# FFN's first quad on Trainium2: VectorE's weight sums moved ahead of f's last three channel blocks, the fourth low part moved ahead of the next sums

## The chip, the cores and the metric

The program runs on one core of a Trainium2 chip. The metric is the device time of one execution in microseconds. Each engine (TensorE, VectorE, ScalarE, GpSimd, and SyncE, which issues the DMAs) has its own queue of instructions, worked in order; semaphores tie the queues together. TensorE's clock is granted at one of two levels, 1.2 and 2.4 GHz.

## The reference, cut to what matters

The reference is a transformer block (latent attention beside an mLSTM, an FFN, a gated embedding) and a second block with a pooling mixer, all in float32, for 1024 tokens of width 1024. The change lies in the FFN of the first block:

```
f = rms_norm(h, ffn_pre_norm)                       # 1024 x 1024
f = (silu(f @ w_gate) * (f @ w_up)) @ w_down        # hidden width 2816 = 11 groups of 256
h = h + rms_norm(f, ffn_post_norm)
```

## The kernel before, in words

**Precision.** Every float32 matrix is used as a high part (rounded by a copy to TensorE's format, fp32r) and a low part (the value less its high part). A product is three matmuls, high x high, high x low, low x high (`three`, line 1356 for all its matmuls). A tile named `_hi` or `_lo` is such a part; `ring_hi`, `ring_lo` are eight slots of weight blocks.

**Strassen's scheme.** The FFN's first two matrix products go by groups of 256 hidden columns: a gate part and an up part for each. Group 0 is done plainly (`whole_quad`, four banks of 24 matmuls, for gate and again for up). From group 1 on each part is a "quad" of seven products in the Winograd form of Strassen's scheme (`quad`), 12 matmuls each: product o takes weight block o from ring slot o and the operand `factors[o]`, which is a quarter of f or one of four sums of quarters, `f_sum[0]` to `f_sum[3]`. Products 0, 4 and 5 use quarters of f, products 1, 2, 3 and 6 use the sums 1, 0, 2 and 3. Each quad also needs four sums of weight quarters (`w_sum`), one for each of its products 1, 2, 3 and 5. The prediction counts products and blocks of a quad from 1 to 7; in the code they are o = 0 to 6.

**Who does what around the change (some 495 to 550 us).** TensorE does group 0's two whole quads, then without a break the gate quad of group 1 and its up quad. VectorE first computes the f sums, in four channel blocks k = 0 to 3: four sums high + low (line 3179), then `f_raw[0]`, `[2]`, `[1]`, `[3]` of that block (lines 3190 to 3195). ScalarE copies the high parts of sums 1, 0, 2 block by block (line 2375), 12 copies in all, and once bank 6 of the whole quads is full the high part of `f_raw[3]` in one copy of 2048 columns (line 2380). The low parts, 2048 columns each, are shared: GpSimd has that of sum 2 (line 1243), VectorE those of sums 1, 0 (line 3203) and 3 (line 3212). All wait for ScalarE's 12 copies or the thirteenth.

VectorE's order is: f's sums for k = 0 to 3; `weight_sums(2, 0)`, the four weight sums of the gate quad (lines 3163 to 3168, each 512 columns); low parts 1 and 0; `weight_sums(3, 1)`, those of the up quad; the first two of group 0's four products silu(gate) x up, which read a PSUM bank (line 3208); low part 3; the other two products; then the sums over the gate quad's own banks (`quad_sums`). `weight_sums` waits for the raw weights' DMA (`raw_in`), and the first of them also until the last rows of f have been transposed, since it writes where these lay.

GpSimd's order is: the low part of sum 2, then for the gate quad block after block (`product_blocks`): a high part (line 1211) and a low part (line 1212) of 512 columns each into a ring slot, when the slot is free and, for a summed block, when its sum is done. Then the up quad's blocks, and so on. The ring's slots are freed by TensorE's whole quads.

TensorE waits ahead of product o of a quad for weight block o (`w_split`), for the gate quad of group 1 also for a count of low parts (`fs_split`), and from the fifth product on for ScalarE's copy of the bank that it adds to. ScalarE's first such copy (line 2385) waits for all four low parts, since it writes where `f_raw[3]` lay. SyncE stores the four products of group 0 to memory when they are done and loads the next raw weights when GpSimd has split the blocks of the last ones.

Of the kernel before, what the change touches and what calls it, by code (L numbers as in the profile page):

```python
# [18 lines left out]
F32 = mybir.dt.float32  # L19
# [3 lines left out]
ALU = mybir.AluOpType  # L23
# [61 lines left out]
def build(nc, a, out):  # L85
    ctx = ExitStack()
    with ctx:
# [10 lines left out]
        def at(name, shape, offset, dt=F32):  # L98
            return nc.alloc_sbuf_tensor_at(name, shape, dt, offset=base + offset)
# [20 lines left out]
        def col(n):  # L120
# [117 lines left out]
            for j, name in enumerate(("e_buf", "d_t", "inter", "s_t", "q_in", "k_w")))  # L238
# [12 lines left out]
        f_sum = [(at(f"fs_hi{i}", [P, 4, HALF], o, F32R), at(f"fs_lo{i}", [P, 4, HALF], o + 8 * KB, F32R))  # L251
                 for i, o in enumerate(f_sum_at)]
        f_raw = [at(f"fs_raw{i}", [P, 4, HALF], o + 8 * KB) for i, o in enumerate(f_sum_at)]
# [132 lines left out]
        fs_raw, fs_hi_ready, fs_split = map(sem, ("fs_raw", "fs_hi_ready", "fs_split"))  # L386
# [49 lines left out]
        US_SUMS, US_PARTS, US_ROWS = 16, 4, 0  # L436
# [154 lines left out]
        def raw_landed(t):  # L591

            return 32 if t == 0 else 32 * (t // 2) if t % 2 == 0 else 32 * ((t - 1) // 2 + 2)
# [2092 lines left out]
        def dve_program(dve):  # L2686
            v = nc.vector
            own = dve_own
# [470 lines left out]
            def block_sums(q, dst, t):  # L3159

                s = [dst[:, i, :].rearrange("p (k n) -> p k n", k=4) for i in range(4)]
                w00, w01, w10, w11 = (wblock(t, c, k) for c in range(2) for k in range(2))
                v.tensor_tensor(s[0], w10, w11, ALU.add).then_inc(w_summed, 1)
                dve.wait_ge(w_summed, IN_SUMS + 4 * q + 1)
                v.tensor_tensor(s[1], s[0], w00, ALU.subtract).then_inc(w_summed, 1)
                v.tensor_tensor(s[2], w00, w10, ALU.subtract).then_inc(w_summed, 1)
                dve.wait_ge(w_summed, IN_SUMS + 4 * q + 2)
                v.tensor_tensor(s[3], w01, s[1], ALU.subtract).then_inc(w_summed, 1)

            def weight_sums(t, r):  # L3170

                dve.wait_ge(raw_in[1 - r], IN_LANDED + raw_landed(2 + r) + 32 * ((t - 2 - r) // 2))
                if r == 0:
                    dve.wait_ge(rows_full, 16 + 2 * TB)
                block_sums(t - 2, w_sum[r], 2 + r)
# [7 lines left out]
            for k in range(4):  # L3183
# [13 lines left out]
                    own.mark(ins)  # L3197
                else:
                    ins.then_inc(fs_raw, 1)
            weight_sums(2, 0)  # L3200
            dve.wait_ge(fs_hi_ready, US_PARTS + 12)
            for i in (1, 0):
                v.tensor_tensor(f_sum[i][1][:], f_raw[i][:], f_sum[i][0][:].bitcast(F32), ALU.subtract).then_inc(fs_split, 1)
            weight_sums(3, 1)
            for j, b in enumerate((2, 3, 0, 1)):
                dve.wait_ge(std_full, 5 + j)
                dve.wait_ge(silu_ready, b + 1)
                v.tensor_tensor(hid_pair[0][:, b, :], ps[:, 4 + b, :], silu_g[:, b, :], ALU.mult).then_inc(hid_ready, 1)
                if j == 1:
                    dve.wait_ge(fs_hi_ready, US_PARTS + 13)  # L3210
                    dve.wait_ge(own.sem, own.at)
                    v.tensor_tensor(f_sum[3][1][:], f_raw[3][:], f_sum[3][0][:].bitcast(F32), ALU.subtract).then_inc(fs_split, 1)

            def quad_sums(q, bank0, copies, dst, sums=None, times=None, first=None, low=None):

# [489 lines left out]
        @block.vector  # L3705
        def _(dve):
            dve_program(dve)
# [30 lines left out]
```

## Time and profile before

| | us |
|---|---|
| median of 3 runs | 1812.74 (1812.66 to 1813.11) |
| the profiled execution | 1813.23 |
| its span, first to last instruction | 1811.4 |
| TensorE busy | 1791.5 (99%) |
| VectorE busy | 1405.5 (78%) |
| GpSimd busy | 1087.2 (60%) |
| ScalarE busy | 691.2 (38%) |

The rows further down name PE for TensorE, PEld for its weight loads, DVE for VectorE, ACT for ScalarE, POOL for GpSimd and SPq for SyncE's DMA queue. A timeline row has the start in us, the recorded length in us (of all instructions merged in the row, xN), engine, line, operation, output tiles <- input tiles with their shapes, and in brackets how long the engine stood idle before and who released it. An instruction's recorded length includes time in which it is held up after its start. Ends of matmuls are modelled: 0.39 us are recorded where the next one starts 0.23 later.

### The profile page before, as it was taken

To read this page: it belongs to the slowest core of one execution; us is meant where nothing else is said; L and a number is where in the kernel's file an instruction comes from. 1 tells how busy PE (TensorE), PEld (TensorE's weight loads), DVE (VectorE), ACT (ScalarE), POOL (GpSimd) and SP (SyncE) were. 2 spreads that over 40 slices of the span, in tenths; PEclk is the share of its full clock that TensorE was granted. 3 is DMA by queue.
4 is the path that set the end of the run, shared out by engine and by line. 5 is a ranking of instruction groups with operands and counts; after the bars stand their busy time and mean duration, and the time that the engine had idled before them with its cause. 6 is when DMAs were issued, how large, how long until landed. Compare 5 with 4: busy or idle time off the path is not lost.

```text
span 1811.4 us, 22601 instructions
## 1 busy us (share of the span) xinstructions
PE 1791.5 (99%) x8518; PEld 1499.4 (83%) x8518; DVE 1405.5 (78%) x1624; ACT 691.2 (38%) x1213; POOL 1087.2 (60%) x766
## 2 busy tenths in 40 slices
PE   9999999999999999999999999999999999999998
PEld 8888888888888888888888888888888888888887
DVE  7889866666696758666599989578888875798897
ACT  6545577843321111111243334415433343333313
POOL 4066632260359988888778878632665465567554
PEclk9999999999999999999999999999999999999999
DMA  7342410032303323243374631113332231943222
GB/s 208 97 150 56 136 23 20 15 129 93 123 29 105 117 82 117 69 140 117 105 278 175 232 128 47 47 47 119 114 117 105 105 139 71 365 168 108 75 97 93
DMA packets 126974, 206.54 MB, mean 114 GB/s; under 512 B 32129, under 2 KB 88065, under 8 KB 123153
## 3 DMA queue, kind: packets, MB, share of 16 engines
q1 hardware_dynamic: 126690, 205.03, 33.0%
q8 instruction: 68, 1.11, 0.2%
q14 instruction: 40, 0.33, 0.1%
q10 hardware_dynamic: 176, 0.07, 0.0%
HBM read 151.51 MB, written 53.04 MB: 113 GB/s over the span
## 4 chain that ended last, share of the span: by engine, by line
PE 72%; DVE 5%; POOL 1%; issue 1%; ACT 1%; DVEq 0%; POOLq 0%
PE ps L1356 64%; PE ps L1705 2%; PE ps L1707 2%; PE ps L1706 2%; DVE y L3609 1%; PE ps L1945 1%; PE ps L1943 1%; PE ps L1944 1%; POOL ring_lo L1212 1%; POOL ring_hi L1211 0%; DVE y L3602 0%; PE ps L1820 0%; DVE xs_lo L3436 0%; PE ps L1692 0%; PE ps L1584 0%
## 5 line engine op out<-in xcount | busy, mean ns | idle before, releaser
L1356 PE MATMUL ps<-f_hi,ring_hi 128*128 128x512 f32 x384 | 149.7, 390 | 1.3 <-POOL ring_lo L1212 1.3
L1356 PE MATMUL ps<-f_hi,ring_lo 128*128 128x512 f32 x384 | 149.4, 389 | 0.0
L1356 PE MATMUL ps<-f_lo,ring_hi 128*128 128x512 f32 x384 | 149.4, 389 | 0.0
L1290 POOL TENSOR_TENSOR ring_lo<-w_sum,ring_hi 128x512 fp32r<-128x512 f32 x60 | 94.4, 1584 | 50.9 <-ACT ring_hi L2512 50.9
L1212 POOL TENSOR_TENSOR ring_lo<-w_sum,ring_hi 128x512 fp32r<-128x512 f32 x80 | 117.9, 1473 | 6.7
L1356 PE MATMUL ps<-d_w_hi,d_hid_hi 128*128 128x512 f32 x312 | 121.5, 390 | 0.3 <-DVE hid L3302 0.3
L1356 PE MATMUL ps<-d_w_hi,d_hid_lo 128*128 128x512 f32 x312 | 121.4, 389 | 0.0
L1356 PE MATMUL ps<-d_w_lo,d_hid_hi 128*128 128x512 f32 x312 | 121.4, 389 | 0.0
L2385 ACT ACTIVATE f_copy<-ps 128x512 f32<-128x512 f32 x60 | 35.4, 597 | 221.2 <-PE ps L1356 202.4
L1356 PE MATMUL ps<-xs_hi,ring_hi 128*128 128x512 f32 x256 | 100.0, 391 | 1.5 <-DVE xs_lo L3436 1.4
L1356 PE MATMUL ps<-xs_lo,ring_hi 128*128 128x512 f32 x256 | 99.6, 389 | 0.0
L1356 PE MATMUL ps<-xs_hi,ring_lo 128*128 128x512 f32 x256 | 99.6, 389 | 0.0
L1356 PE MATMUL ps<-fs_hi,ring_hi 128*128 128x512 f32 x240 | 93.5, 390 | 0.0
L1356 PE MATMUL ps<-fs_lo,ring_hi 128*128 128x512 f32 x240 | 93.4, 389 | 0.0
L1356 PE MATMUL ps<-fs_hi,ring_lo 128*128 128x512 f32 x240 | 93.4, 389 | 0.0
L1211 POOL TENSOR_SCALAR ring_hi<-w_sum 128x512 fp32r<-128x512 f32 x80 | 72.7, 908 | 32.1 <-PE ps L1356 31.5
L1211 POOL TENSOR_SCALAR ring_hi<-stage 128x512 fp32r<-128x512 f32 x38 | 33.2, 874 | 89.4 <-PE ps L1707 83.3
L1356 PEld LDWEIGHTS ps<-f_hi,ring_hi 128*128 128x128 f32 x384 | 72.1, 188 | 16.9 <-POOL ring_lo L1212 1.9
L1356 PEld LDWEIGHTS ps<-f_hi,ring_lo 128*128 128x128 f32 x384 | 72.1, 188 | 15.0
L1356 PEld LDWEIGHTS ps<-f_lo,ring_hi 128*128 128x128 f32 x384 | 72.1, 188 | 14.9
L1290 POOL TENSOR_TENSOR ring_lo<-stage,ring_hi 128x512 fp32r<-128x512 f32 x24 | 35.4, 1475 | 76.0 <-ACT ring_hi L2512 76.0
L1094 POOL TENSOR_TENSOR w_lo<-stage,w_hi 128x1024 fp32r<-128x1024 f32 x30 | 75.5, 2518 | 2.5
(560 smaller groups left out, 5807.4 us busy)
## 6 DMA issues: line engine op xcount, KB each, us to landing
d_raw<-hid_rows SPq DMA_DIRECT2D x37, 512.0 KB, 4.4
stage<-in_w_up SPq DMA_DIRECT2D x22, 512.0 KB, 4.7
wd_raw<-in_w_down SPq DMA_DIRECT2D x22, 512.0 KB, 5.4
raw_w<-in_w_gate SPq DMA_DIRECT2D x20, 512.0 KB, 4.9
stage<-in_pool_w_in SPq DMA_DIRECT2D x16, 512.0 KB, 5.0
raw_w<-in_pool_w_in SPq DMA_DIRECT2D x16, 512.0 KB, 4.8
m_rows<-u_row SPq DMA_DIRECT2D x16, 512.0 KB, 2.6
z_rows<-z_buf SPq DMA_DIRECT2D x8, 1024.0 KB, 4.1
```

The costliest lines, as they stand in the source:

```text
L1094: g.tensor_tensor(lo, stage[:, h, :], hi.bitcast(F32), ALU.subtract).then_inc(parted[h], 1)
L1211: pool_hi.do(pool, g.tensor_scalar(view(hi), src, 1.0, 0.0, ALU.mult, ALU.add))
L1212: g.tensor_tensor(view(lo), src, view(hi).bitcast(F32), ALU.subtract).then_inc(w_split, 1)
L1290: g.tensor_tensor(as_blocks(lo, src), src, as_blocks(hi, src).bitcast(F32), ALU.subtract).then_inc(w_split, 1)
L1356: last = mm(out_ap, l, r, start=(start and j == 0), stop=(stop and j == n - 1), skip_group_check=onto)
L1705: mm(o, l_hi, w_hi[s][:, c:c + HALF], start=(k == 0), stop=False)
L1706: mm(o, l_hi, w_lo[s][:, c:c + HALF], start=False, stop=False)
L1707: last = mm(o, l_lo, w_hi[s][:, c:c + HALF], start=False, stop=(k == 7))
L1943: mm(ps[:, m, :], w_hi[1][:, c:c + P], x_h, start=(k == 0), stop=False)
L1944: mm(ps[:, m, :], w_hi[1][:, c:c + P], x_l, start=False, stop=False)
L1945: last = mm(ps[:, m, :], w_lo[1][:, c:c + P], x_h, start=False, stop=(k == 3))
L2385: f(copies[:, j, :], ps[:, bank0 + bank_of[o], :], ACT.Copy).then_inc(prod_copied, 1)
```

## The change

In VectorE's program `weight_sums(2, 0)` moves from behind all f sums to behind those of channel block 0. Low part 3 moves from between the four products to right behind low parts 1 and 0. `weight_sums(3, 1)` moves behind the four products. VectorE now also waits, ahead of the low parts, until its last f sum has landed. No other engine's program is changed.

```diff
@@ dve_program, from line 3196
                     own.mark(ins)
                 else:
                     ins.then_inc(fs_raw, 1)
-            weight_sums(2, 0)
+                if k == 0:
+                    weight_sums(2, 0)
+            dve.wait_ge(fs_raw, US_SUMS + 13)
             dve.wait_ge(fs_hi_ready, US_PARTS + 12)
             for i in (1, 0):
                 v.tensor_tensor(f_sum[i][1][:], f_raw[i][:], f_sum[i][0][:].bitcast(F32), ALU.subtract).then_inc(fs_split, 1)
-            weight_sums(3, 1)
+            dve.wait_ge(fs_hi_ready, US_PARTS + 13)
+            dve.wait_ge(own.sem, own.at)
+            v.tensor_tensor(f_sum[3][1][:], f_raw[3][:], f_sum[3][0][:].bitcast(F32), ALU.subtract).then_inc(fs_split, 1)
             for j, b in enumerate((2, 3, 0, 1)):
                 dve.wait_ge(std_full, 5 + j)
                 dve.wait_ge(silu_ready, b + 1)
                 v.tensor_tensor(hid_pair[0][:, b, :], ps[:, 4 + b, :], silu_g[:, b, :], ALU.mult).then_inc(hid_ready, 1)
-                if j == 1:
-                    dve.wait_ge(fs_hi_ready, US_PARTS + 13)
-                    dve.wait_ge(own.sem, own.at)
-                    v.tensor_tensor(f_sum[3][1][:], f_raw[3][:], f_sum[3][0][:].bitcast(F32), ALU.subtract).then_inc(fs_split, 1)
+            weight_sums(3, 1)
```

## Rows read from the trace of the kernel before

**Rows 1.** The page, busy time, share of the span and instructions by engine.

```profile
PE 1791.5 (99%) x8518; PEld 1499.4 (83%) x8518; DVE 1405.5 (78%) x1624; ACT 691.2 (38%) x1213; POOL 1087.2 (60%) x766
```

**Rows 2.** TensorE's waits, whole run: waited for, total us, times, longest.

```profile
PE ps L1598 <- DVE probs L3028: 3.1, 6, 1.0
...
PE ps L1356 <- POOL ring_lo L1212: 1.3, 2, 1.0
```

**Rows 3.** Chain of waits in order of time: start, us, what.

```profile
494.13 27.25 PE ps L1356 x120
...
521.48 4.74 POOL fs_lo L1243
...
544.41 95.74 PE ps L1356 x421
```

**Rows 4.** Timeline of VectorE around the change: start, us, line, tiles.

```profile
504.15 0.69 DVE L3195 TENSOR_TENSOR fs_raw<-f_tmp,fs_raw 128x512 f32<-128x512 f32 x1
...
504.88 2.50 DVE L3179 TENSOR_TENSOR f_tmp<-f_hi,f_lo 128x512 f32<-128x512 f32 x4
...
520.33 0.69 DVE L3163 TENSOR_TENSOR w_sum<-raw_w 128x512 f32<-128x512 f32 x1
...
521.05 0.69 DVE L3165 TENSOR_TENSOR w_sum<-w_sum,raw_w 128x512 f32<-128x512 f32 x1
...
527.71 5.99 DVE L3203 TENSOR_TENSOR fs_lo<-fs_raw,fs_hi 128x2048 fp32r<-128x2048 f32 x2
...
535.43 0.98 DVE L3165 TENSOR_TENSOR w_sum<-w_sum,stage 128x512 f32<-128x512 f32 x1
...
539.05 1.27 DVE L3208 TENSOR_TENSOR hid<-ps,silu_g 128x512 f32<-128x512 f32 x2
...
540.24 2.27 DVE L3212 TENSOR_TENSOR f_lo<-fs_raw,f_hi 128x2048 fp32r<-128x2048 f32 x1
```

**Rows 5.** Timeline of GpSimd, the same stretch.

```profile
535.96 1.60 POOL L1212 TENSOR_TENSOR ring_lo<-w_sum,ring_hi 128x512 fp32r<-128x512 f32 x1
...
540.24 2.75 POOL L1211 TENSOR_SCALAR ring_hi<-raw_w 128x512 fp32r<-128x512 f32 x1
...
547.04 0.62 POOL L1211 TENSOR_SCALAR ring_hi<-raw_w 128x512 fp32r<-128x512 f32 x1
...
547.75 1.29 POOL L1212 TENSOR_TENSOR ring_lo<-raw_w,ring_hi 128x512 fp32r<-128x512 f32 x1
```

**Rows 6.** Timeline of ScalarE, f's last high parts.

```profile
519.72 1.68 ACT L2375 ACTIVATE fs_hi<-fs_raw 128x512 fp32r<-128x512 f32 x3 [3.03 <-DVE fs_raw L3193]
...
521.78 1.90 ACT L2380 ACTIVATE f_hi<-fs_raw 128x2048 fp32r<-128x2048 f32 x1
```

**Rows 7.** Timeline of SyncE's queue: the raw gate weights.

```profile
494.23 0.92 SPq L827 DMA_DIRECT2D raw_w<-in_w_gate  x2
```

**Rows 8.** Timeline, VectorE released by ScalarE.

```profile
582.84 0.60 ACT L2385 ACTIVATE f_copy<-ps 128x512 f32<-128x512 f32 x1 [2.12 <-PE ps L1356]
...
583.47 1.10 DVE L3224 TENSOR_TENSOR f_copy<-f_copy 128x512 f32<-128x512 f32 x1 [3.23 <-ACT f_copy L2385]
```

**Rows 9.** Timeline, VectorE and GpSimd starting almost together.

```profile
782.01 0.69 DVE L3163 TENSOR_TENSOR w_sum<-raw_w 128x512 f32<-128x512 f32 x1 [3.76 <-DMA raw_w<-in_w_gate]
...
782.03 1.15 POOL L1211 TENSOR_SCALAR ring_hi<-w_sum 128x512 fp32r<-128x512 f32 x1
```

**Rows 10.** Timeline of TensorE, first matmul of product 2.

```profile
534.90 0.50 PE L1356 MATMUL ps<-fs_hi,ring_hi 128*128 128x512 f32 x1
```

**Rows 11.** Windows: us, busy (count) by engine, granted clock, DMA share, GB/s.

```profile
3.00:4.00 1.00, 1.00 (x7) 1.00 (x6) 0.00 (x0) 0.00 (x0) 0.94 (x16) 1.00 1.03 388
...
5.00:6.00 1.00, 1.00 (x12) 1.00 (x11) 0.00 (x0) 0.97 (x4) 0.00 (x0) 1.00 1.05 375
...
1804.00:1805.00 1.00, 0.75 (x4) 0.29 (x2) 0.38 (x2) 0.00 (x0) 0.00 (x0) 1.00 0.00 0
...
1806.50:1807.00 0.50, 0.00 (x0) 0.00 (x0) 0.50 (x1) 0.50 (x2) 0.00 (x0) 0.95 0.00 0
```

## The prediction

> **What bounds the kernel now.** I read the page first, then TensorE's waits, then the chain of waits in order of time, then the timelines of VectorE, ScalarE and GpSimd around the change. TensorE is busy for 99% of the span [rows 1]: time is gained only by closing its gaps and lost by opening one. Its waits are few; the longest single ones are 1.0 us [rows 2], and one of these is the place of this change, where product 5 of the first gate quad waits for GpSimd's low part. The chain shows the same stretch: TensorE's whole quads, GpSimd's low part of f_sum[2] at 521.48, GpSimd's weight blocks, and from 544.41 TensorE alone with 421 matmuls in 95.74 us, 0.227 us each [rows 3]. So from 521.5 to 544.4 the path runs through GpSimd, and what happens to it there is passed on to the end: behind it TensorE has no long wait left in which a delay could vanish.
>
> GpSimd and VectorE hold each other up. VectorE's sum at 521.05 ends at 521.74; GpSimd's 2048-column low part ends at 526.22, 4.48 later, with 4.74 recorded [rows 3, 4]. VectorE's 2048-column low part at 540.24 takes 2.27 and GpSimd's copy of the same start takes 2.75 and ends 0.48 after it, where the one at 547.04 takes 0.62 [rows 4, 5]. GpSimd's low part at 535.96 takes 1.60, not 1.29, and ends 1.15 after VectorE's sum (535.43 + 0.98 = 536.41) [rows 4, 5]. The pattern: one runs, the other is recorded from its start but works only when the first has ended, and then they alternate. VectorE's products that read PSUM (539.05, two in 1.27) are not held up [rows 4].
>
> **Part 1, the weight sums moved behind channel block 0.** Four sums leave the place behind f's last sum and enter behind 504.15. Their price is the spacing of the same four today: 0.72 to the second (520.33 to 521.05) and 0.61 for each other [rows 4]; with GpSimd idle there they run free, 0.72 + 3 x 0.61 = 2.55. Today the next instruction waits 0.73 for the previous sum to land (504.15 to 504.88), of which the moved sums cover 0.12. Net 2.43 us. Everything behind is f's sums of blocks 1 to 3, so the last of them, and ScalarE's last high parts that they release, move from 521.40 to 523.83 [rows 6]. Both VectorE's and GpSimd's low parts wait for exactly this. Nothing hides it: ScalarE stands idle between the blocks. The raw weights are there by then: SyncE issued them at 494.23 [rows 7], ten us ahead; no DMA moves. Bounds of this term: 2.43 free, 4 x 0.61 + 0.72 = 3.2 with one more wait; I take 2.43.
>
> **Part 2, three low parts together, in front of GpSimd's first block.** Today VectorE's 2048-column low parts come at 527.71 [rows 4], when GpSimd's 4.74 us low part is done, and the fourth at 540.24, which alone costs GpSimd 2.1 us of its block 5. In the new order the release at 523.83 starts both engines. VectorE starts 0.03 after a ScalarE end (582.84 + 0.60, then 583.47) [rows 8], GpSimd 0.08 after (521.40, then 521.48) [rows 3, 6]. In the near tie at 782.01 against 782.03 the engine that started first kept its natural 0.69 and the other took 1.15 [rows 9]. So VectorE goes first, and they alternate:
> - VectorE low part 1: 523.86 to 526.13 (2.27).
> - GpSimd low part of f_sum[2]: to 530.61 (+4.48).
> - VectorE low part 0: to 532.8 (2.15 behind a release: 2.27 less the 0.1 of its start).
> - GpSimd block 1's high part: to 533.2 (+0.48).
> - VectorE low part 3: to 535.4 (+2.15). Its high part is no obstacle: it takes ScalarE 1.90 and ends near 526.3 [rows 6].
> - GpSimd block 1's low part: to 536.5 (+1.15).
>
> TensorE's first product of this quad needs that block. The product at 534.90 is the second one [rows 10]; 12 matmuls of 0.227 ahead of it put the first at 532.1. It now starts at 536.6, behind a gap of 4.5 us.
>
> **What comes back.** The weight sums of the next quad now stand behind VectorE's four products and meet GpSimd's blocks 3 and 4: each low part goes from 1.29 to 1.60 and each high part from 0.62 to 1.06 [rows 5]. GpSimd ends block 2 at 538.5, block 3 near 541.2, block 4 near 543.9, block 5 near 545.9. TensorE asks for them from 539.3 on in steps of 2.73, product 5 at 536.6 + 48 x 0.227 + 0.1 (restart) = 547.6. So no block is late again, and today's waits ahead of product 5 (1.0 and its restart) go away. Today product 5 starts at 544.41, by its steady rate 544.5. Net: **+3.1 us**. ScalarE's copies are released earlier (by low part 3 at 535.4, not 542.5), which no one on the path waits for. In SyncE's queue the stores of the four products are released earlier, and the next raw loads with GpSimd's last block of this quad, about 1 us later; I cost this at nothing, since the sums on them stand a whole quad (7 x 2.73 = 19 us) ahead of TensorE's need. The up quad's weight sums, done by 542.8, are needed by GpSimd only behind the gate quad's seven blocks.
>
> **Part 3, the clock.** Nothing in this trace shows a gap as long as 4.5 us inside the kernel. The nearest rows are its two ends. Behind the last matmul (busy 0.75 of the slice, so until 1804.75) the granted clock is 0.95 over 1806.5 to 1807, so it fell from the upper level (2.4 GHz) to the lower one at about 1806.95, 2.2 us after TensorE stopped [rows 11]. At the start TensorE did 7 matmuls in one us and two us later 12 (128 columns each) [rows 11]; it began at 1.0, so it spent 3 to 4 us slow. With a gap of twice the 2.2 us I expect a fall inside it. Price: from 0, if it doesn't fall, to half of twice the start's stretch, 3.7 us; I take half of 3.7 us of slow work, 1.85 us, the start's stretch being the nearest. Sum 3.1 + 1.85 = **+5.0 us**. The Trainium skill (TensorE: Matmul & The Clock Gate, Part 1) says that the lower level is the default and that recent activity alone holds the upper one. By that rule the gap costs twice, once as a gap and once in what follows it; without the rule the sum would be 3.1. The end of this trace agrees with it; no stretch inside the kernel tests it.
>
> The profiled execution took 1813.23, 0.49 above the median 1812.74, with a span of 1811.4; the difference is added to the median: 1812.74 + 5.0 = **1817.7**.
>
> **Rivals.**
> - **The clock stays up.** Only the +3.1 remains: 1815.9. For it: no fall inside the kernel was ever seen. Against: 2.2 us of rest sufficed at the end.
> - **GpSimd wins the tie.** Then its low part runs 523.9 to 528.4, VectorE's to 530.5 and 533.2, block 1's low part comes between them and ends at 534.3; TensorE restarts after 2.3 us, block 2 is ready at 538.3 and costs 1.2 again, and product 5 lies 2.1 later than today: 1814.8, or some 1816.7 if the clock falls too. Against it: 0.03 against 0.08 us of start.
> - **Not slower: GpSimd never waited for the high parts.** The chain puts TensorE's bank 6 (494.13 + 27.25 = 521.38) ahead of GpSimd's low part [rows 3]. If that was the real release, the 2.43 is hidden from GpSimd. It then starts at 521.4 on its own, holds VectorE off until 526, and the fourth low part no longer stands in block 5: the 1.1 us at 544 go, plus the few tenths around: 1811.5. It decides at whether GpSimd starts before 522. Against it: its wait names the twelve high parts, ScalarE's last ends at 521.40, also 0.08 ahead.
> - **More goes wrong**: two slow stretches or a late block as well, +7: 1820.
>
> **Numbers.** Forecast 0.57; clock stays 0.20; GpSimd first 0.10; not slower 0.08; more 0.05. A difference of 0.2% (3.6 us) is about what can be told from no change here. Slower by over 0.2%: 0.57 + 0.05 + 0.04 of the tie's case = 0.66. Within: 0.20 + 0.06 + 0.05 = 0.31. Faster by over 0.2% would need more than TensorE's idle time here gives: 0.03. The range: below, the tie's 1814.8 less half a us for the lengths that I rounded; above, +3.1 and 3.7 of clock, 1819.6, and a little: 1814.2 to 1820.0.
>
> **What would show it.** VectorE's four weight sums at 504.8 to 507.3; ScalarE's last high part at 523.8; VectorE's low part natural at 2.27 and GpSimd's at some 6.7; the fourth low part ended at 535.4; TensorE idle 532.1 to 536.6; in the windows behind it a granted clock of 0.50 for 3 to 4 us; product 5 not waiting. Wrong if TensorE's gap there is under 3 us, or if the matmuls behind it keep 0.227.

## The result and the profile after

| | us |
|---|---|
| before, median of 22 runs | 1812.96 (1812.53 to 1814.46) |
| changed, median of 22 runs | 1815.49 (1815.05 to 1816.37) |
| ratio, 95% interval | 1.0014 (1.0008 to 1.0020) |
| changed, profiled execution and its span | 1815.29, 1813.2 |
| predicted | 1817.7, range 1814.2 to 1820.0 |

The change costs 2.5 us: slower, as forecast in direction, inside the range, and half of the forecast +5.0. It fell into what the prediction calls within 0.2%. The profiled executions differ by 1815.29 - 1813.23 = 2.06.

TensorE's waits over the whole run, columns as in [rows 2]:

```profile
PE ps L1356 <- POOL ring_lo L1212: 3.3, 3, 2.1
PE ps L1598 <- DVE probs L3028: 3.1, 6, 1.0
```

GpSimd's low parts now cost TensorE 3.3 us in three waits where they cost 1.3 in two. The timeline of the changed kernel, here engine after engine (VectorE, GpSimd, ScalarE, TensorE), shows where (these answer to [rows 3 to 6] and [rows 10]; line 3205 is now the low parts 1 and 0, 3208 low part 3):

```profile
503.73 0.69 DVE L3195 TENSOR_TENSOR fs_raw<-f_tmp,fs_raw 128x512 f32<-128x512 f32 x1
504.34 0.68 DVE L3163 TENSOR_TENSOR w_sum<-raw_w 128x512 f32<-128x512 f32 x1
...
506.88 2.49 DVE L3179 TENSOR_TENSOR f_tmp<-f_hi,f_lo 128x512 f32<-128x512 f32 x4
...
523.48 9.36 DVE L3205 TENSOR_TENSOR fs_lo<-fs_raw,fs_hi 128x2048 fp32r<-128x2048 f32 x2 [1.08 <-ACT fs_hi L2375]
532.77 3.34 DVE L3208 TENSOR_TENSOR f_lo<-fs_raw,f_hi 128x2048 fp32r<-128x2048 f32 x1
523.45 4.63 POOL L1243 TENSOR_TENSOR fs_lo<-fs_raw,fs_hi 128x2048 fp32r<-128x2048 f32 x1 [21.50 <-ACT fs_hi L2375]
528.03 2.67 POOL L1211 TENSOR_SCALAR ring_hi<-raw_w 128x512 fp32r<-128x512 f32 x1
530.79 3.17 POOL L1212 TENSOR_TENSOR ring_lo<-raw_w,ring_hi 128x512 fp32r<-128x512 f32 x1
533.93 2.66 POOL L1211 TENSOR_SCALAR ring_hi<-w_sum 128x512 fp32r<-128x512 f32 x1
536.67 1.27 POOL L1212 TENSOR_TENSOR ring_lo<-w_sum,ring_hi 128x512 fp32r<-128x512 f32 x1
521.70 1.67 ACT L2375 ACTIVATE fs_hi<-fs_raw 128x512 fp32r<-128x512 f32 x3 [3.03 <-DVE fs_raw L3193]
531.57 0.39 PE L1356 MATMUL ps<-f_hi,ring_lo 128*128 128x512 f32 x1
534.11 0.47 PE L1356 MATMUL ps<-f_hi,ring_hi 128*128 128x512 f32 x1 [2.15 <-POOL ring_lo L1212]
...
538.00 0.50 PE L1356 MATMUL ps<-fs_hi,ring_hi 128*128 128x512 f32 x1 [0.93 <-POOL ring_lo L1212]
```

The reader is to see four things. The moved weight sums run free: they take 504.34 to 506.88, where line 3179 stood directly behind block 0's last sum in [rows 4]. ScalarE's last high parts end at 521.70 + 1.67 = 523.37. GpSimd starts at 523.45 and is recorded with 4.63, little more than the 4.48 that the prediction has for it once VectorE is out of the way: it was first. VectorE starts at 523.48, 0.03 later, and its two low parts take 9.36 together, not 5.99 as in [rows 4]. And TensorE rests twice: from the end of the whole quads (531.57 + 0.23 = 531.80) to 534.11, 2.3 us, and ahead of product 2 for 1.1. Product 5 no longer waits. I compare stretches by their distance from TensorE's last transposes (line 1692; 493.04 before, 492.75 changed), since the executions differ by some 0.3 us ahead of it: the up quad's second product starts 62.40 us after them before the change, 64.43 in the changed kernel, +2.03. Before (first fence), then changed:

```profile
493.04 1.09 PE L1692 MATMUL ps<-ident,f_blk 128*128 128x128 f32 x8 [0.27 <-DVE f_blk L3151]
531.65 3.20 POOL L1212 TENSOR_TENSOR ring_lo<-w_sum,ring_hi 128x512 fp32r<-128x512 f32 x1
555.44 0.39 PE L1356 MATMUL ps<-fs_hi,ring_hi 128*128 128x512 f32 x1
```

```profile
492.75 1.09 PE L1692 MATMUL ps<-ident,f_blk 128*128 128x128 f32 x8 [0.31 <-DVE f_blk L3151]
557.18 0.39 PE L1356 MATMUL ps<-fs_hi,ring_hi 128*128 128x512 f32 x1
```

It is in part chance that 2.03 is near the 2.06 between the profiled executions: their spans differ by 1.8 (1813.2 - 1811.4), since the changed one was 0.3 ahead at the transposes.

The sum can be followed at GpSimd. Its low part starts 2.3 later after the transposes (30.70, not 28.44). Its block 2 is ready 3.4 later: at 536.67 + 1.27 = 537.94, 45.2 after them, where it was 531.65 + 3.20 = 534.85, 41.8 after them. The other 1.1 is low part 3, which now stands among its turns. Before the change product 2 had no time to spare: it began at 534.90 [rows 10], 0.05 behind its block. Against these 3.4 stands product 5's wait of 1.2 (from 543.02 + 0.23 to 544.41), which is gone: 2.2, near the 2.03.

### The profile page after: what moved, and what is told of

Same layout as the page of the kernel before. It is cut to its first block, busy times and chain, and to the rows that moved or that the text cites. A ratio compares the mean times of both kernels' runs of the same rounds, so it can differ in the third digit from the quotient of the medians.

```text
span 1813.2 us, 22602 instructions
## 1 busy us (share of the span) xinstructions
PE 1792.3 (99%) x8518; PEld 1500.5 (83%) x8518; DVE 1406.6 (78%) x1624; ACT 692.0 (38%) x1213; POOL 1085.9 (60%) x766
## 4 chain that ended last, share of the span: by engine, by line
PE 70%; DVE 5%; issue 2%; POOL 2%; ACT 1%; DMA 0%; DVEq 0%; SPq 0%; POOLq 0%
PE ps L1356 63%; PE ps L1705 1%; PE ps L1707 1%; PE ps L1706 1%; POOL ring_lo L1212 1%; POOL ring_hi L1211 1%; DVE y L3610 1%; PE ps L1945 1%; PE ps L1943 1%; PE ps L1944 1%; DVE y L3603 0%; PE ps L1820 0%; DVE xs_lo L3437 0%; PE ps L1584 0%; PE ps L1692 0%
```

## The experiments

**Which part costs.** e2_low_parts_only and e3_sums_only each have one half of the change; both keep the added wait for VectorE's last f sum.

```diff
 # e2_low_parts_only, against the changed kernel
-                if k == 0:
-                    weight_sums(2, 0)
+            weight_sums(2, 0)
             dve.wait_ge(fs_raw, US_SUMS + 13)
```

> Only the second part of the change: the gate quad's weight sums stand behind all of f's sums as before; the three low parts stand together and the up quad's weight sums behind the four products as in the changed kernel. Theory (the loss is the delay of f's sums by the moved weight sums): GpSimd's low part starts at 521.5 as before, block 1 is in time, block 3 waits for low part 3 and product 3 comes 1.2 us late, product 5 does not wait: total within 0.3 us of the kernel before. Rival (the loss is the pile of low parts in front of GpSimd's first blocks): about as slow as the changed kernel, +2 us or more.

Measured: 1813.05 against 1813.02 before, ratio 1.0001 (0.9992 to 1.0010). TensorE has one gap in this stretch (its waits, 500 to 550; then GpSimd's block 3):

```profile
PE ps L1356 <- POOL ring_lo L1212: 1.0, 1, 1.0
```

```profile
521.69 4.75 POOL L1243 TENSOR_TENSOR fs_lo<-fs_raw,fs_hi 128x2048 fp32r<-128x2048 f32 x1 [19.11 <-ACT fs_hi L2375]
...
535.03 2.67 POOL L1211 TENSOR_SCALAR ring_hi<-w_sum 128x512 fp32r<-128x512 f32 x1
537.78 1.27 POOL L1212 TENSOR_TENSOR ring_lo<-w_sum,ring_hi 128x512 fp32r<-128x512 f32 x1
```

GpSimd starts in time and is held up by low part 3 in block 3's high part (2.67 at 535.03) instead of in block 5's [rows 5]; a gap of 1.0 moved from product 5 to product 3. As the theory said, the pile of low parts alone costs nothing.

```diff
 # e3_sums_only, against the kernel before
+                if k == 0:
+                    weight_sums(2, 0)
-            weight_sums(2, 0)
+            dve.wait_ge(fs_raw, US_SUMS + 13)
             dve.wait_ge(fs_hi_ready, US_PARTS + 12)
```

> Only the first part of the change: the gate quad's weight sums behind f's channel block 0; low parts, products and the up quad's weight sums in the order of before (with the wait for VectorE's last f sum ahead of low part 1). Theory (delay of f's sums): GpSimd's low part starts at 523.5 to 523.9, block 1 is ready near 534.2, TensorE's gap ahead of product 1 is 2.2 us; low part 3 stands in GpSimd's block 4 or 5, so product 4 comes 1.1 us late; total +2.0 us on the kernel before, as the changed kernel. Rival (pile of low parts): within 0.3 us of the kernel before.

Measured: 1815.56, ratio 1.0014 (1.0005 to 1.0022), the time of the changed kernel. The first gap ends here:

```profile
534.64 0.67 PE L1356 MATMUL ps<-f_hi,ring_hi 128*128 128x512 f32 x1 [2.70 <-POOL ring_lo L1212]
```

It is 2.9 us in the profiled execution (from 531.55 + 0.23), 2.3 in another; product 4 was not late, since behind both the clock fell and GpSimd caught up (below). So the whole loss comes with the weight sums ahead of f's last three blocks. This move does two things at once: f's sums end later, and VectorE's low parts meet GpSimd's block 1 instead of block 2. No run separates the two.

**Who is first at the port.** The prediction had VectorE first. e1_vector_first makes it so: one of the four products goes into VectorE's idle time, and only one wait is left directly ahead of the low parts. `first_products(j, b)` is the body of the loop over the products, with its two waits.

```diff
 # e1_vector_first, against the changed kernel
             dve.wait_ge(fs_raw, US_SUMS + 13)
+            first_products(0, 2)
             dve.wait_ge(fs_hi_ready, US_PARTS + 12)
...
-            for j, b in enumerate((2, 3, 0, 1)):
...
+            for j, b in ((1, 3), (2, 0), (3, 1)):
+                first_products(j, b)
```

> The changed kernel, with the first of VectorE's four products (it reads PSUM) moved into VectorE's idle time ahead of the low parts, so that only one wait stands directly ahead of low part 1. Theory (port taken in turns, the first to start keeps it): VectorE now starts about 0.03 us after ScalarE's last high part and GpSimd 0.08 after; low part 1 runs at its natural 2.27, GpSimd's low part of sum 2 is recorded with some 6.7, block 1 of the gate quad is ready 2.0 us later than in the changed kernel, TensorE's gap ahead of it grows from 2.3 to about 4.3 us and the gap ahead of product 2 (1.1) goes: +0.9 us against the changed kernel, about 1816.4 (+3.4 on before). If the clock falls in the longer gap, another 1 to 3.5 us and a granted clock of 0.50 behind it. Rival (the two engines share evenly, so the order of the tie does not matter, only the total of work ahead of the block): same time as the changed kernel within 0.3 us. Second rival (VectorE is 0.11 late for another reason than its two waits in a row): GpSimd still starts first and nothing changes.

Measured: 1817.95, ratio 1.0028 (1.0017 to 1.0038), 2.5 us above the changed kernel. Its timeline, engine after engine, then windows (us, busy of TensorE, granted clock, DMA share, GB/s):

```profile
521.95 1.68 ACT L2375 ACTIVATE fs_hi<-fs_raw 128x512 fp32r<-128x512 f32 x3 [3.03 <-DVE fs_raw L3193]
523.66 8.91 DVE L3211 TENSOR_TENSOR fs_lo<-fs_raw,fs_hi 128x2048 fp32r<-128x2048 f32 x2 [0.29 <-ACT fs_hi L2375]
523.70 6.71 POOL L1243 TENSOR_TENSOR fs_lo<-fs_raw,fs_hi 128x2048 fp32r<-128x2048 f32 x1 [21.51 <-ACT fs_hi L2375]
...
533.13 3.17 POOL L1212 TENSOR_TENSOR ring_lo<-raw_w,ring_hi 128x512 fp32r<-128x512 f32 x1
531.76 0.39 PE L1356 MATMUL ps<-f_hi,ring_lo 128*128 128x512 f32 x1
536.45 0.77 PE L1356 MATMUL ps<-f_hi,ring_hi 128*128 128x512 f32 x1 [4.30 <-POOL ring_lo L1212]
537.01 0.63 PE L1356 MATMUL ps<-f_lo,ring_hi 128*128 128x512 f32 x1
537.44 0.63 PE L1356 MATMUL ps<-f_hi,ring_lo 128*128 128x512 f32 x1
```

```profile
535.00:536.00 1.00, 0.00 (x0) 1.00 0.00 0
536.00:537.00 1.00, 0.55 (x1) 0.53 0.00 0
...
538.00:539.00 1.00, 1.00 (x4) 0.50 1.02 410
539.00:540.00 1.00, 1.00 (x4) 0.76 1.00 406
540.00:541.00 1.00, 1.00 (x6) 1.00 0.43 164
```

This is the prediction's own forecast, step by step: VectorE 0.03 behind ScalarE's end (521.95 + 1.68 = 523.63), GpSimd's low part recorded with 6.71, block 1 ready at 533.13 + 3.17 = 536.3, TensorE idle for 4.5 us, and behind the gap a granted clock of 0.50 with matmuls 0.43 apart instead of 0.23, until about 539.5. The price of both together was forecast at +5.0 on before. By the medians it is 1817.95 - 1813.02 = +4.9, by the trace +4.4 (the up quad's second product comes 66.82 us after the transposes, not 62.40).

e7_two_waits adds nothing but a second, long met wait:

```diff
 # e7_two_waits, against e1_vector_first
             first_products(0, 2)
+            dve.wait_ge(fs_raw, US_SUMS + 13)
             dve.wait_ge(fs_hi_ready, US_PARTS + 12)
```

> e1_vector_first with one thing added: behind the hoisted product VectorE waits once more for its last f sum, which has long landed, directly ahead of its wait for ScalarE's high parts. No work and no real waiting is added. Theory (two waits in a row make the instruction behind them start later even if the first is met long before): VectorE starts 0.11 us after ScalarE's end instead of 0.03, GpSimd with its 0.08 is first, its low part is recorded with 4.6, TensorE's gap ahead of product 1 is 2.3 us, and the time falls from 1817.9 to that of the changed kernel, 1815.5, by 2.4 us. Rival (VectorE was early in e1 because it had just been working, not because of the number of waits): VectorE starts 0.03 after and everything is as in e1, 1817.9.

Measured: 1815.59, ratio 1.0014 (1.0005 to 1.0023), 2.4 us less than e1_vector_first. Its timeline, engine after engine:

```profile
521.66 1.68 ACT L2375 ACTIVATE fs_hi<-fs_raw 128x512 fp32r<-128x512 f32 x3 [3.03 <-DVE fs_raw L3193]
523.41 4.62 POOL L1243 TENSOR_TENSOR fs_lo<-fs_raw,fs_hi 128x2048 fp32r<-128x2048 f32 x1 [21.51 <-ACT fs_hi L2375]
523.44 9.36 DVE L3212 TENSOR_TENSOR fs_lo<-fs_raw,fs_hi 128x2048 fp32r<-128x2048 f32 x2 [0.36 <-ACT fs_hi L2375]
```

ScalarE ends at 523.34; GpSimd follows by 0.07, VectorE by 0.10. An empty wait makes the kernel faster by 2.4 us, because it makes VectorE lose a tie that it had better lose. All that the two kernels differ in is this wait. The 2.4 us hold two things, the block that is ready sooner and the clock, which fell in e1_vector_first's profiled execution and stayed up in this one.

**The clock.** In the changed kernel's first profiled execution the gap of 2.3 us left the clock up. Two more executions:

> The changed kernel once more, for its clock record. In the profile at hand TensorE's gap of 2.3 us left the granted clock up and the stretch is 2.06 us longer than before, where the medians differ by 2.5. Theory (the gap is long enough for a fall in some executions, by where it lies): some further execution shows a granted clock of 0.50 behind the gap and is 0.5 to 1.7 us longer. Rival (this gap never lowers the clock): 1.00 throughout, and the 0.5 us lie elsewhere.

> The changed kernel a third time, as the one before: a granted clock of 0.50 behind the gap in some execution, or 1.00 in all of them.

Windows of TensorE in the changed kernel (first fence) and in a2_changed_again (second), columns as above:

```profile
531.00:534.00 3.00, 0.96 (x5) 1.00 0.00 0
534.00:537.00 3.00, 2.89 (x12) 1.00 0.00 0
537.00:540.00 3.00, 2.07 (x10) 1.00 0.22 87
```

```profile
531.00:534.00 3.00, 1.09 (x5) 1.00 0.00 0
534.00:537.00 3.00, 2.63 (x8) 0.74 0.00 0
537.00:540.00 3.00, 3.00 (x11) 0.69 0.13 53
```

The gap is 2.4 us in a2_changed_again and the clock fell behind it, for some 3.4 us; in a3_changed_third it stayed up behind 2.3 us. The fall costs little: while TensorE works slowly, GpSimd finishes block 2, and the second gap of 1.1 us disappears. The up quad's second product comes 64.97 us after the transposes, against 64.43 and 64.45 without a fall: 0.5 us. So the changed kernel loses 2.0 in this stretch in some executions and 2.6 in others. Whole executions do not show it: a2_changed_again took 1815.99, 0.7 more than the first, as expected, but a3_changed_third without a fall took 1816.10, the longest of the three. Its transposes came at 493.65, 0.9 later than in the first.

> The kernel with the first part alone once more: there a gap of 2.7 us was followed by 3.4 us at a granted clock of 0.50. Theory (it depends on where the gap lies in the execution): the fall may be missing here, and the execution is then some 1.7 us shorter. Rival (2.7 us always suffice): the same fall again.

e3b_sums_again (1815.33 as a whole) had the fall again, behind a gap of only 2.3 us, and was 0.6 us shorter than e3_sums_only's profiled execution in the same stretch (64.78 against 65.38); the theory of a missing fall is not borne out there. How long a gap must be cannot be read from these: 2.3 us did it in this execution and not in the changed kernel's first and third, nor in that of e7_two_waits.

**Taking GpSimd's blocks out of the way.** In both kernels GpSimd is idle from 503 to its low part. e4_pool_blocks_early keeps VectorE's changed order and lets GpSimd split blocks 1 to 3 there. `fs_split` counts VectorE's three low parts alone in it; product 4 is ordered behind GpSimd's low part by its weight block.

```diff
 # e4_pool_blocks_early, against the changed kernel
-            def product_blocks(t, r, slots_free):
+            def product_blocks(t, r, slots_free, blocks=range(7)):
...
+            product_blocks(2, 0, std_slots_free, range(3))
             pool.wait_ge(fs_hi_ready, US_PARTS + 12)
-            g.tensor_tensor(f_sum[2][1][:], ..., ALU.subtract).then_inc(fs_split, 1)
-            product_blocks(2, 0, std_slots_free)
+            pool_hi.mark(g.tensor_tensor(f_sum[2][1][:], ..., ALU.subtract))
+            product_blocks(2, 0, std_slots_free, range(3, 7))
...
-                    pe.wait_ge(fs_split, US_PARTS + {1: 2, 2: 3, 3: 3, 6: 4}[o])
+                    pe.wait_ge(fs_split, US_PARTS + {1: 1, 2: 2, 3: 2, 6: 3}[o])
...
-                    act.wait_ge(fs_split, US_PARTS + 4)
+                    act.wait_ge(fs_split, US_PARTS + 3)
```

> The changed kernel, but GpSimd splits blocks 1 to 3 of the gate quad in its idle time ahead of the low part of sum 2 (the weight sums stand early enough for that). Theory: GpSimd's three blocks cost VectorE's f sums about 1.6 us each by turns at the port (4 to 5 us in all), so the last high part comes near 528; products 1 to 3 no longer wait for blocks, product 2 waits up to 1 us for low part 1: total 0.1 to 0.5 us below the kernel before, some 2.5 us below the changed one. Rival (f's sums then end so late that low part 1 sets product 2, with low part 0 and block 4 late behind it): 1 to 3 us above the kernel before.

Measured: 1812.01 against 1813.02 before, ratio 0.9995 (0.9986 to 1.0004). Its 11 runs lie from 1811.61 to 1812.89, those of before from 1812.59 to 1813.78; the interval of the ratio still holds 1, so a gain is not shown by it; the 1.0 us is what the medians say, and the trace has 1.4 (below). Both are more than the 0.1 to 0.5 expected. It has the lowest median of all kernels here. GpSimd's timeline:

```profile
505.05 0.62 POOL L1211 TENSOR_SCALAR ring_hi<-raw_w 128x512 fp32r<-128x512 f32 x1 [2.97 <-PE ps L1357]
...
514.19 1.61 POOL L1212 TENSOR_TENSOR ring_lo<-w_sum,ring_hi 128x512 fp32r<-128x512 f32 x1
527.79 4.62 POOL L1244 TENSOR_TENSOR fs_lo<-fs_raw,fs_hi 128x2048 fp32r<-128x2048 f32 x1 [11.99 <-ACT fs_hi L2376]
...
541.04 1.30 POOL L1212 TENSOR_TENSOR ring_lo<-raw_w,ring_hi 128x512 fp32r<-128x512 f32 x1
```

GpSimd's low part starts 4.3 us later than in the changed kernel, since its early blocks hold up VectorE's f sums, and TensorE waits for nothing in 500 to 550: the up quad's second product comes 60.99 us after the transposes, 1.4 less than before.

e6_block1_early asks whether VectorE's changed order has a share in that: VectorE as before, GpSimd's block 1 alone early.

```diff
 # e6_block1_early, against the kernel before; fs_split counted as in e4_pool_blocks_early
+            product_blocks(2, 0, std_slots_free, range(1))
             pool.wait_ge(fs_hi_ready, US_PARTS + 12)
...
-            product_blocks(2, 0, std_slots_free)
...
+            product_blocks(2, 0, std_slots_free, range(1, 7))
```

> The kernel before with VectorE's order untouched; GpSimd alone splits block 1 of the gate quad (raw weights, no sum) in its idle time near 505, ahead of the low part of sum 2. Theory: the block costs VectorE's f sums some 1.6 us by turns at the port and takes 2.7 us out of GpSimd's path behind them, so 0.5 to 1.1 us of the 1.16 us gap ahead of product 5 go: 0.5 to 1.0 us below the kernel before. If it reaches the time of e4, VectorE's changed order is not needed for that gain. Rival (e4's gain needs three blocks out of the way, since a delay of f's sums counts in full): no gain, or slower by up to 0.5 us.

Measured: 1813.48 against 1812.94, ratio 1.0003 (0.9994 to 1.0012): no gain. The theory failed. TensorE's wait in 500 to 550, then VectorE's low part 3:

```profile
PE ps L1357 <- ACT f_copy L2386: 1.6, 1, 1.6
```

```profile
541.49 2.27 DVE L3213 TENSOR_TENSOR f_lo<-fs_raw,f_hi 128x2048 fp32r<-128x2048 f32 x1
```

GpSimd is out of the way as meant, and product 5 waits all the same, now for ScalarE's copy of bank 0, which waits for low part 3. VectorE's f sums were held up by GpSimd's block, and with them low part 3 between the products: it starts 48.60 us after the transposes (541.49 - 492.89), not 47.20 (540.24 - 493.04, [rows 4]). Two limits stood one behind the other at product 5. In the kernel before ScalarE's copy began at 542.55 and took some 0.6, and product 5 was due at 543.02 + 0.23 = 543.25: low part 3 had almost nothing to spare, and it came 1.4 later here. In e4_pool_blocks_early, which has low part 3 early, the second limit does not show. That this half of the change is what pays there is argued, not shown: e4_pool_blocks_early differs from e6_block1_early also in where the weight sums stand and in blocks 2 and 3, and low part 3 early with block 1 early alone was not tried.

## Why the prediction was right or wrong

- **What bounds the stretch: right.** The kernels run here differ on the path from f's sums through ScalarE and GpSimd to TensorE; in e6_block1_early alone ScalarE's copy behind low part 3 came last.
- **Part 1, +2.43 us on f's sums: right.** From block 0's last sum to the next instruction on f it is 506.88 - 503.73 = 3.15, not 0.73: 2.42. f's last sum, and ScalarE's last high parts with it, starts 28.95 us after the transposes (521.70 - 492.75), not 26.68 (519.72 - 493.04, [rows 6]): 2.3. e3_sums_only carries the whole loss.
- **Part 2, the turns at the port: right as a mechanism, wrong in who begins.** The failed step is "So VectorE goes first". It rested on VectorE's 0.03 us [rows 8], taken from an instruction behind another pattern of waits. The change puts two waits in a row ahead of low part 1; with that the start is 0.11 behind ScalarE's end, and GpSimd's 0.08 wins. The case was among the rivals, at 0.10, with +2.1 as its price; +2.03 was traced. e1_vector_first and e7_two_waits show that the order alone, with the fall of the clock that it brings, separates 1817.95 from 1815.59. So the measured time lies in the range by this rival's price, which set its lower end; the forecast's own sum of +5.0 was not met in the changed kernel.
- **What comes back: right.** Products 3 to 5 do not wait, product 2 waits 1.1 (the rival had 1.2).
- **Part 3, the clock: right in the case it was worked out for.** Behind the 4.5 us gap of e1_vector_first the clock fell. It cost some 1.4 us, not 1.85: product 1's twelve matmuls took 540.70 - 536.45 = 4.25, where 12 x 0.227 and 0.1 of restart are 2.8. The 3.7 us behind the 1.85 came from the start of the run, where [rows 11] show matmuls at a slow pace but a granted clock of 1.00; that the clock made them slow was inferred there. In the case that came, the gap of 2.3 us sometimes suffices; the rival's 1816.7 with a fall was too dear, since the second gap takes up most of the slow work. The Trainium skill (TensorE: Matmul & The Clock Gate, Part 1) has the upper level held by recent activity alone. The 0.50 behind the gaps of e1_vector_first and a2_changed_again agrees.
- **The rival "not slower": refuted.** GpSimd's start moved with ScalarE's last high part, by 2.3 us; the chain's bank 6 [rows 3] was a coincidence of 0.02 us.
- **The chances.** Two thirds on slower by over 0.2% followed from the tie. A 0.05 us difference read from an instruction with other waits was no ground for 0.57 against 0.10.
- **What stays open.** 0.5 us of the medians' 2.5 lies beyond the traced 2.03. Executions with a fall may hold a part of it; how often the clock falls was not counted. But the medians also lie 0.3 to 0.4 above the trace in e2_low_parts_only (0.0 against -0.2), e4_pool_blocks_early (-1.0 against -1.4) and e6_block1_early (+0.5 against +0.2), where TensorE has no gap above 2 us. All are set against the one profiled execution of the kernel before, which took 0.27 more than its median, so the falls need not be the cause.

## What to carry to other kernels

Work moved ahead of a chain delays everything behind it by nearly its full length (2.42 of 2.55 us here), even where it runs "free" there: look at what the chain releases, not at the idle engine beside it. Where VectorE and GpSimd wait for the same event and VectorE's instruction reads two SBUF operands, as its low parts do, work out who starts first, from instructions with the same number of waits, and price both orders. When one late block gates a stretch, look for the next limit behind it before moving the first.

## What was not expected of the hardware

- VectorE behind two waits in a row started its low part 1 0.10 to 0.11 us after ScalarE's recorded end (in the changed kernel's three executions, e3_sums_only, e3b_sums_again, e4_pool_blocks_early and e7_two_waits), behind a single one 0.03 (e1_vector_first; [rows 8] for another instruction), though the first of the two had been met about a microsecond before. GpSimd's low part started 0.07 to 0.08 after it in all of them.
- A gap of TensorE of 2.3 to 2.9 us was followed by some 3.4 us at a granted clock of 0.50 in three of six profiled executions that had one (a2_changed_again, e3_sums_only, e3b_sums_again; not in the changed kernel's first and third execution and e7_two_waits). Each matmul took 0.43 us there instead of 0.23.
